# Value products of a block attention: probabilities as the stationary operand, or values

## What is computed

```python
def _masked_softmax(s, mask, axes):
    s = jnp.where(mask, s.astype(jnp.float32), NEG_INF)
    m = jnp.max(s, axis=axes, keepdims=True)
    e = jnp.where(mask, jnp.exp(s - m), 0.0)
    return e / jnp.maximum(jnp.sum(e, axis=axes, keepdims=True), TINY)
...
        p_c = _masked_softmax(s_c, m_c, (-1,))
        o_c = jnp.einsum('bqgrn,bngd->bqgrd', p_c.astype(vc.dtype), vc)
...
        p_s = _masked_softmax(s_s, m_s, (-2, -1))
        o_s = jnp.einsum('bqgrks,bqgksd->bqgrd', p_s.astype(v_sel.dtype), v_sel)
...
        p_w = _masked_softmax(s_w, m_w, (-1,))
        o_w = jnp.einsum('bqgrk,bkgd->bqgrd', p_w.astype(v_w.dtype), v_w)
        return gt[..., 0:1] * o_c + gt[..., 1:2] * o_s + gt[..., 2:3] * o_w
```

## Time and profile before

| | us |
|---|---|
| median of 3 runs | 3366.2 (3365.84 to 3368.9) |
| the profiled execution, its own time | 3376.0 |
| its span in the trace | 3374.2 |
| TensorE busy / share of the span | 3157.1 / 94% |
| VectorE busy | 1226.1 / 36% |
| ScalarE busy | 472.2 / 14% |
| GpSimd busy | 666.9 / 20% |
| mean granted clock of TensorE | 0.858 of 2.4 GHz |

### The profile page before, as it was taken

How to read it: one execution, slowest core, us unless ns; L and a number is a source line. 1 busy time by engine, 2 the same in 40 slices (tenths; PEclk the granted TensorE clock), 3 DMA queues, 4 the chain that set the end, 5 groups by cost and what they waited for, 6 DMA issues and landing times.

```text
span 3374.2 us, 40264 instructions
## 1 busy us (share of the span) xinstructions
PE 3157.1 (94%) x16373; PEld 2839.4 (84%) x16373; DVE 1226.1 (36%) x2069; ACT 472.2 (14%) x692; POOL 666.9 (20%) x359
## 2 busy tenths in 40 slices
PE   8988786999999989999999999997989999999996
PEld 8987554667766678899999999887979999999994
DVE  4995125333323211523322222385152222332224
ACT  3020112111111110400000000142040000000002
POOL 3430000000000012222232222132203222223220
PEclk9987766555555569999999999998999999999998
DMA  4105530000000021011111111011101111111101
GB/s 151 51 19 154 134 112 0 0 1 1 0 0 1 0 91 38 26 44 44 37 50 44 44 44 44 25 44 38 38 19 48 46 44 44 44 37 47 46 19 53
DMA packets 82859, 145.11 MB, mean 43 GB/s; under 512 B 26382, under 2 KB 54286, under 8 KB 82446
## 3 DMA queue, kind: packets, MB, share of 16 engines
q1 hardware_dynamic: 60126, 129.68, 12.2%
q10 hardware_dynamic: 22640, 14.16, 1.5%
HBM read 134.88 MB, written 13.07 MB: 44 GB/s over the span
## 4 chain that ended last, share of the span: by engine, by line
PE 85%; DVE 10%; ACT 2%; issue 2%; DMA 1%; SPq 1%; DVEq 0%; ACTq 0%
PE PS L556 43%; PE PS L836 7%; PE PS L537 5%; PE PS L542 5%; PE PS L541 5%; PE PS L820 3%; PE PS L825 2%; PE PS L805 2%; DVE CA L1300 2%; PE PS L647 2%; PE PS L821 2%; PE PS L607 1%; DVE Y L1470 1%; PE PS L758 1%; PE PS L824 1%
## 5 line engine op out<-in xcount | busy, mean ns | idle before, releaser
L556 PE MATMUL PS<-XH,WH 128*128 128x364 f32 x3048 | 681.9, 332 | 59.6 <-ACTq L988 16.3
L516 POOL CAST WH<-RAW 128x1024 fp32r<-128x1024 f32 x177 | 200.0, 1130 | 2582.7 <-PE PS L556 1362.0
L556 PE MATMUL PS<-XH,WL 128*128 128x364 f32 x3048 | 677.8, 331 | 0.0
L556 PE MATMUL PS<-XL,WH 128*128 128x364 f32 x3048 | 677.8, 331 | 0.0
L556 PEld LDWEIGHTS PS<-XH,WH 128*128 128x128 f32 x3048 | 535.7, 190 | 63.0 <-issue 39.9
L556 PEld LDWEIGHTS PS<-XL,WH 128*128 128x128 f32 x3048 | 534.9, 190 | 0.0
L556 PEld LDWEIGHTS PS<-XH,WL 128*128 128x128 f32 x3048 | 534.8, 190 | 0.0
L518 POOL TENSOR_TENSOR WL<-RAW,WH 128x1024 fp32r<-128x1024 f32 x177 | 464.5, 2624 | 14.2
L1648 DVE TENSOR_TENSOR HT<-SL,PS 128x1092 f32<-128x1092 f32 x44 | 56.9, 1292 | 867.9 <-PE PS L556 851.2
L537 PE MATMUL PS<-HH,WH 128*128 128x364 f32 x1056 | 351.4, 333 | 15.5 <-DVE HL L1654 8.1
L542 PE MATMUL PS<-HL,WH 128*128 128x364 f32 x1056 | 348.3, 330 | 0.0
(11 more groups left out here) (243 smaller groups left out, 2657.5 us busy)
## 6 DMA issues: line engine op xcount, KB each, us to landing
RAW<-wst SPq DMA_DIRECT2D x174, 512.0 KB, 3.4
KVP<-cache SPq DMA_DIRECT2D x64, 128.0 KB, 2.2
XRAW<-xT SPq DMA_DIRECT2D x8, 546.0 KB, 10.7
Y<-xT SPq DMA_DIRECT2D x8, 546.0 KB, 7.7
yT<-Y ACTq DMA_DIRECT2D x3, 1456.0 KB, 9.7
PG<-cache SPq DMA_DIRECT2D x64, 64.0 KB, 2.3
PG<-cache ACTq DMA_DIRECT2D x64, 64.0 KB, 2.3
win_old<-win_past SPq DMA_DIRECT2D x1, 4032.0 KB, 17.4
```

The costliest lines, as they stand in the source:

```text
L516: pool.tensor_copy(WH[:, s, :], RAW[:, s, :]).then_inc(hi_done, 1)
L556: mm = pe.matmul(PS[:, 3 * bank_set + c, 0:CH], w, x[:, k, c * CH:(c + 1) * CH], start=(q == 0 and w is hi and x is XH), stop=(q == len(ks ...
```

## The change

The two operands of a value product change places. The stationary operand is now a 128-column slice of the values and ones of both groups, `[:, g:g + P]` of the 130 columns; for group 0 the result has its 64 features on partitions 0 to 63 and the sum on 64, for group 1 the sum on 63 and the features on 64 to 127. The moved operand is the whole `PT` buffer of the step, 512 columns. A step issues one such product instead of four. The rows that belong to the other group are computed and not used.

The result stands with features on partitions. At the last step of a branch ScalarE copies the bank to a new buffer `OT` (`move_out`), and a new kind of unit, `ov`, turns it back with four 128 x 128 transposes into the banks of the units; `mix` reads it there. There are 32 `ov` units, two for a phase, at the head of the next phase's units (an even phase has ov WINDOW, ov SELECTED, out, cmp, cmpv, then the maxima; an odd one the same without out). The waits for `p_mixw` and `p_mixed` ahead of a branch's first product become waits for `p_ot`. VectorE now follows `flow`.

```diff
+    OT = place("OT", [P, 2, R * P], F32, pb_at)
...
+            todo = [("cmpv", m)] + (maxima(m + 1) if m + 1 < N_PH else [])
+            if m:
+                todo.insert(0, ("ov", m - 1, WINDOW))
+                todo.insert(2, ("ov", m - 1, SELECTED))
+                if m % G == 0:
+                    todo.insert(3, ("out", m // G - 1))
+                todo.insert(4 if m % G == 0 else 3, todo.pop(1))
...
+        ending = [("ov", N_PH - 1, WINDOW), ("ov", N_PH - 1, SELECTED), ("out", QT_N - 1)]
...
+        def turned_out_of(m, kind):
+            return 2 * m + 1 + (kind == SELECTED)
...
+                elif kind == "ov":
+                    pe.wait_ge(p_ot, turned_out_of(m, item[2]))
+                    for r in range(R):
+                        mm = pe.transpose(PS[:, b, r * P:(r + 1) * P], OT[:, item[2], r * P:(r + 1) * P], ident)
...
                 if begin and m:
-                    pe.wait_ge(p_mixw if kind == WINDOW else p_mixed, m)
-                for r in range(R):
-                    mm = pe.matmul(PS[:, 6 if kind == WINDOW else 7, r * (HD + 1):(r + 1) * (HD + 1)],
-                                   PT[:, n % 4, r * P:(r + 1) * P], VNAT[:, kind, kb, g, :],
-                                   start=(begin and r == 0), stop=(end and r == R - 1))
+                    pe.wait_ge(p_ot, turned_out_of(m - 1, kind))
+                mm = pe.matmul(PS[:, 6 if kind == WINDOW else 7, :],
+                               VNAT[:, kind, kb, :, :].rearrange("p g d -> p (g d)")[:, g:g + P], PT[:, n % 4, :],
+                               start=begin, stop=end)
                 mm.then_inc(p_v, 1)
...
+            def move_out(n):
+
+                m, kind, _ = steps[n]
+                if n == last_step[m, kind]:
+                    act.wait_ge(p_v, n + 1)
+                    if m:
+                        act.wait_ge(a_full, unit_of["ov", m - 1, kind] + 1)
+                    act.activation(OT[:, kind, :], PS[:, 6 if kind == WINDOW else 7, :], ACT.Copy).then_inc(p_ot, 1)
...
                 if n + 1 < N_STEPS:
                     exps(n + 1)
+                if n:
+                    move_out(n - 1)
                 for item in between[n]:
-                    if item != ("out", QT_N - 1):
-                        empty(item)
+                    empty(item)
+            move_out(N_STEPS - 1)
...
             def mix(m, kind):
 
-                dve.wait_ge(p_v, last_step[m, kind] + 1)
-                acc = PS[:, 6 if kind == WINDOW else 7, 0:R * (HD + 1)].rearrange("p (r d) -> p r d", r=R)
-                link(dve.reciprocal(ST[:, 240:244], acc[:, :, HD]))
+                b = room(("ov", m, kind))
+                g = m % G
+                acc = PS[:, b, :].rearrange("p (r d) -> p r d", r=R)
+                link(dve.reciprocal(ST[:, 240:244], acc[:, :, HD - g]))
```

More of the change, by code:

```diff
@@ L240, in build @@
                         for n, name in enumerate(("CAUSR", "FARR", "IDR"))]
+    OT = place("OT", [P, 2, R * P], F32, pb_at)
     PT = place("PT", [P, 4, R * P], F32, pb_at + size(2, 1056))
-    assert size(CT, CH) + size(R * MR) + 3 * size(P) <= size(2, 1056) and size(1024) <= size(CT, CH)
+    assert size(CT, CH) + size(R * MR) + 3 * size(P) <= size(2, 1056) and size(2, R * P) <= size(CT, CH)
     RSC = place("RSC", [P, NCH, CH], F32, r_t + 3 * size(TP))
@@ L354, in build @@
                 between[first_step[m, WINDOW] + n * j // len(todo)].append(item)
-        between[-1].append(("out", QT_N - 1))
-        flow = maxima(0) + [item for items in between for item in items]
+        ending = [("ov", N_PH - 1, WINDOW), ("ov", N_PH - 1, SELECTED), ("out", QT_N - 1)]
+        flow = maxima(0) + [item for items in between for item in items] + ending
         unit_of = {item: u for u, item in enumerate(flow)}
@@ L852, in _ @@
                 for item in between[n]:
-                    if item != ("out", QT_N - 1):
-                        unit(item)
+                    unit(item)
                 values(n)
-            unit(("out", QT_N - 1))
+            for item in ending:
+                unit(item)
             pe.wait_ge(a_dve, taken(("out", QT_N - 1)))
@@ L1573, in mix @@
             def mix(m, kind):
-                dve.wait_ge(p_v, last_step[m, kind] + 1)
-                acc = PS[:, 6 if kind == WINDOW else 7, 0:R * (HD + 1)].rearrange("p (r d) -> p r d", r=R)
-                link(dve.reciprocal(ST[:, 240:244], acc[:, :, HD]))
+                b = room(("ov", m, kind))
+                g = m % G
+                acc = PS[:, b, :].rearrange("p (r d) -> p r d", r=R)
+                link(dve.reciprocal(ST[:, 240:244], acc[:, :, HD - g]))
                 link(dve.tensor_tensor(ST[:, 240:244], ST[:, 240:244], gates(m, 1 + kind), ALU.mult))
                 t = OTMP[:, :].rearrange("p (r d) -> p r d", r=R)
[L1580 to L1584, removed]
+                dve.tensor_tensor(t, acc[:, :, HALF[g]], ST[:, 240:244, None].to_broadcast([P, R, HD]), ALU.mult).then_inc(a_dve, 1)
+                dve.wait_ge(a_dve, taken(("ov", m, kind)))
+                o = OC[:, :, g, :]
+                if kind == WINDOW:
+                    link(dve.tensor_tensor(o, o, t, ALU.add))
+                else:
+                    dve.tensor_tensor(o, o, t, ALU.add).then_inc(p_mixed, 1)
+                    dve.wait_ge(p_mixed, m + 1)
             def out_low(i):
@@ L1610, in _ @@
             side = 0
[L1611 to L1622, removed]
+            for item in flow:
+                kind, m = item[0], item[1]
+                if kind == "cmp":
+                    cmp_scores(m)
+                elif kind == "cmpv":
+                    cmp_values(m)
+                elif kind == "ov":
+                    mix(m, item[2])
+                elif kind == "out" and m < QT_N - 1:
+                    out_low(m)
+                elif kind in (WINDOW, SELECTED):
+                    if item[1:] == (m, 0) and kind == SELECTED:
+                        select(m)
+                    maximum(item)
+                    if kind == WINDOW and item[2] == 1:
+                        cmp_probs(m)
+                    elif item[2] == R - 1:
+                        dve.wait_ge(a_dve, taken(item))
+                        if kind == WINDOW and m >= N_PH - NCH * CONV_STEPS:
+                            conv_scale(side)
+                            side += 1
             assert side == NCH * CONV_STEPS
-            mix(N_PH - 1, SELECTED)
             for c in range(CT):
```

19 lines of the change are left out of this document (1 added, 18 removed).

## The result

The changed kernel takes 3212.7 us (median of 4 runs, 3208.1 to 3230.0) where the kernel before took 3366.7 in the same session: a ratio of 0.955 with a 95% interval of 0.952 to 0.958. That is 154 us faster; 194 were forecast. The profiled execution of after has 3212.2 us, a span of 3210.2 and a mean granted clock of 0.925, against 3374.2 and 0.858.

The account below looks back on a forecast made before the run. PE at half clock was taken to bound the attention stage. Late part -218, work left low +37, early part -15, end +2 gave -194 us, applied to the 3366.2 us median: 3172 us, range 3105 to 3295.

Parts of the forecast that it names:

- What bounds the kernel: Prompt attention, about 548 to 1221 us: PE sets the time, running at 1.2 GHz, half of its 2.4.
- Does the clock rise?: Attention stage: 512-column full-row values and ov transposes bring the high clock in nearly every phase from second or third query tile.
- late part: 674 to 1221 us, 114 steps: 547 us becomes 329 all high, a gain of 218; 15% left low gives 37 back.
- early part: First 126 us of the stage, 18 steps, much of it set by DVE's units: a gain of 15 us, bounds 0 and 50.
- One step at the low clock: Each of 132 steps: new value group 1.84 us against 1.74, +0.10 a step, +13 us.
- At the high clock: One step: value pair 0.97 us with the change of rows, scores 1.09 against 1.74, other PE work at ratio 0.60.
- new waits: ov's waits for ACT's move and for banks, and ACT's for the last product: all cost nothing while DVE is mostly idle.
- Added turns: 32 ov units of four 128x128 transposes on PE, 0.85 us each: +27 us at the low clock.
- The end: After the last exponential, ACT first waits for the last value products and moves them: +2 us.
- (a): Rival, every step: 64-row scores between the values hold the clock at 0.50; +43 us, 3409 us; chance 0.15.
- (b): Rival: clock rises at each phase head and falls at the compressed scores, half the work high; -97, 3269 us; chance 0.18.
- (c): Rival, late phases: DVE or ACT becomes the bound, 5 us in each of 11 phases; -139, 3227 us; chance 0.10.

Follow-up runs that it names:

- w1_wide: The kernel before, with each head's value product moving 128 columns instead of 65, operands not exchanged and nothing turned: 3197.6 us, ratio 0.950.
- n1_narrow: The changed kernel, with each value product moving 128 of the 512 columns from the second query tile on: 3264.5 us, ratio 0.970.
- the other order: The changed kernel with each phase's head units reordered: ov WINDOW, cmp, ov SELECTED, first maximum, (out, second maximum), cmpv, rest: 3157.3 us, ratio 0.938.
- the shifted kernel: The changed kernel with the stage's first four transposes issued four times over, so everything behind starts some 2 us later: 3217.0 us, ratio 0.958.
- w3b_wide_late: w1_wide with one gap left empty ahead of cmp, so that cmp comes one gap later: 3228.3 us, ratio 0.956.
- c2_gap: The changed kernel with one empty gap behind ov WINDOW, cmp staying behind ov SELECTED: 3219.5 us, ratio 0.956.

## Why the prediction was right, and where it was off

**What bounds the kernel** held: PE's clock in this stage was the lever. **Does the clock rise?** held in its main argument, the 512 columns over full rows in place of 65; both runs on the number of columns bear it out. Its second argument, that the `ov` units at the head of a phase lift the clock, wasn't needed: w1_wide has no `ov` units and has the clock, and doubling them gained nothing. Of the signs, PEclk near 9 came only in the last five slices of the stage (8, 9, 8, 8, 9), and the stage took 528 us, not 450 to 490.

The measured time lies 41 us above the forecast: 21 from the late part, 20 from the early part. No two large errors cancelled.

**One step at the low clock** was 1.84 us, as forecast. **At the high clock** it was forecast at 0.97 + 1.09 = 2.06 us and measured 0.95 + 0.99 = 1.94 (776.94 to 778.88): the scores' 1.09 was read from a step with the compressed scores behind it, which hold its last product 0.43 us instead of 0.34. After has the same 1.09 where `cmp` follows (940.17 to 941.26).

**The late part** was forecast at 329 + 37 = 366 us and took 387. A granted clock of 0.85 between 0.5 and 1 means 30% of the time low, 116 us. Against 577 us for the part all low, that is 20% of the work instead of 15: 50 us given back, not 37. PE idled for 17.4 us (387.0 - 369.6), 1.4 before: 16 that the sum had at nothing. That makes 395. The remaining -8 weren't measured by themselves; a step, in the sum at 0.97 + 0.60 x 1.74 = 2.01 us, took 1.94, which over the 91 high ones of 114 is some 6 of them.

So three terms of the sum were mis-sized:

- "All cost nothing", said of the **new waits**. ScalarE was idle, but it was behind in its own list: the copy stands behind the next exponential, and PE came to the turn too soon 15 times, by 0.83 us at the high clock, by 0.41 mostly at the low. With `out` behind `mix` (6.6, of which 1.5 were there before) it is 16.5 us over the stage, and the waits of the maxima (L818) and of `rows` (L804) grew as well, from 7.1 and 4.6 to 10.5 and 6.7 us.
- "15% of this work low, an estimate from the fall at 804 when units of narrow products come (one such unit a phase)". The low time doesn't lie in a short piece of every phase. It lies in whole stretches: 53 us at the head of the late part, 44 in phase 13.
- The **early part**, forecast at -15 us, measured +4 (130 for 126). There the clock rose for moments only (0.57), so the edit's own cost remained: 18 steps x 0.10 and 8 `ov` x 0.85 = 9 us, and waits such as these two, at the low clock, PE timeline of after:

```profile
582.97 1.09 PE L808 MATMUL PS<-CST,OT 128*128 128x128 f32 x4 [0.41 <-ACT OT L1175]
...
585.61 1.09 PE L812 MATMUL PS<-CST,OC 128*128 128x128 f32 x4 [1.55 <-DVE OC L1610]
```

**Added turns** were priced at 27 us low and 14 high; doubling them cost 21.6, in between, with one more late phase at the low clock in it. **The end** was forecast at +2 and came to +1.8: before, 12.85 us from the last exponential to the output projection (1217.65 to 1230.50), now 14.66 (1050.85 to 1065.51). Timeline of after:

```profile
1050.85 0.60 ACT L1146 ACTIVATE PT<-PS 128x512 f32<-128x512 f32 x1 [1.58 <-PE PS L838]
...
1052.66 0.60 ACT L1175 ACTIVATE OT<-PS 128x512 f32<-128x512 f32 x1 [1.22 <-PE PS L848]
...
1065.51 1.28 PE L565 MATMUL PS<-XH,WH 128*128 128x364 f32 x3 [8.47 <-DVE XL L1616]
```

The sum by the trace: -160 late, +4.8 early, +1.0 in the last piece, -154 for the stage. The median agrees. The profiled span shows 164 less, with the 10.8 us that came ahead of the stage by themselves; I had applied the forecast to the median, so they are in neither number.

**The rivals.** (a), the clock stays low, fell. The profile of n1_narrow is its picture: busy PE, clock 0.5. The Trainium skill ("TensorE: Matmul & The Clock Gate", "Part 1: The HAM clock gate") says that activity releases the throttle. Read as busy time, that would let none of these edits move the clock; the clock over the stage is 0.77 in w1_wide for 0.51 before, and 0.51 in n1_narrow for 0.77 in after, so what a busy engine moves matters. (b), flickering with half of the work low, was 3269; the measured case lies between it and the forecast, nearer the forecast, and its place, the fall at the compressed scores, is right for phase 13. (c) didn't occur: PE's idle time at the high clock is single waits for ScalarE's copy and for VectorE's `mix` and maxima, not a full engine; DVE is busy 162 of 387 us.

**Still open**: why the clock comes up when it does in phases 2 to 7, why `cmp` one gap later makes the wide kernel slower, what a fall needs, since `cmp` and a wait came before one together and each alone, and were also passed without one, and which of the moves in the other order does its work. The runs show the effects of places, not a rule that gives the best one.

## What to carry to other kernels

Where TensorE is busy without a gap and its granted clock still reads half, look at what it moves: try giving the narrow products more columns over all rows, even useless ones (169 us here), before cutting work, and expect that trimming a busy stretch can make it slower. Once the clock is up, waits that cost little at half speed grow, and the order of short units can decide whether whole phases stay fast; try a few orders, and shift the start by a microsecond or two to see whether a good one is luck. The other order (3157.3 us) is the fastest of the kernels here, and beats both the kernel before and the changed one.

## What the runs showed of the hardware that I had not expected

- TensorE with nothing but unused columns added ran the stage in 503 us instead of 682; with three quarters of the value products taken out of the changed kernel it lost 52 us.
- A fall can cost far more than the unit beside it: `cmp` lasts 1.4 us, and four low stretches that begin within one us of its end last 37 to 44 us (943.2 in after; 811.0 and 889.5 shifted; 856.5 with the gap). Phase 13 takes 54 us in after (934 to 988) and 34 in the shifted kernel (965 to 999).
- No single neighbour explains the falls: `cmp` with a wait ahead (943.2 in after), `cmp` without one (960.8 in w3b_wide_late) and a wait without `cmp` (952.1 in c2_gap) all came before one.
- Two microseconds of added work at the start moved the low phases from 13 to 9 and 11 and left the median within 4.3 us of what it was.
- Unchanged code ahead of the stage differed by 10.8 us between two profiles, with the clock at 0.64 and 0.91 in the same 20 us window. A difference of that size between two profiled spans says nothing of an edit; the stage has to be cut out of both.
